# Attention, token shift and low-rank products of the first block, placed between the column tiles of the mixer's input projection

## What is computed

```
hn = rms_norm(h, g_mix[l]) * (1.0 + sc2) + sh2
proj = hn @ w_mix_in[l]                      # 1024 -> 2560 columns
p_att, p_rwkv, p_conv = split(proj, ...)     # 768, 1024 and 768 columns
y_att  = sliding_window_sink_attention(p_att, ...)   # 8 query heads, 2 key heads of 64
y_rwkv = rwkv7_time_mix(p_rwkv, ...)         # p = p + mu * (token_shift(p) - p), then a recurrence
y_conv = short_conv_mix(p_conv, conv_w)      # b_gate * conv3(c_gate * h)
h = h + (1.0 + gt2) * concat(y_att, y_rwkv, y_conv) @ w_mix_out[l]
```

## Time and profile before

| what | us |
|---|---|
| median of three runs | 3284.01 |
| the profiled execution, its own time | 3291.0 |
| its span, first to last instruction | 3288.9 |
| TensorE busy | 3033.3 (92%) |
| VectorE busy | 1597.2 (49%) |
| ScalarE busy | 977.7 (30%) |
| GpSimd busy | 228.7 (7%) |
| TensorE on the chain that ended last | 87% |

### The profile page before, as it was taken

One profiled execution on the slowest core, in us unless ns is written; L12 is line 12 of the kernel. 1 busy time (PEld: TensorE's weight loads), 2 busy tenths in 40 slices (PEclk: granted clock), 3 DMA queues, 4 the chain that ended last, 5 costly groups with the idle time before them and its releaser, 6 DMA issues.

```text
span 3288.9 us, 43744 instructions
## 1 busy us (share of the span) xinstructions
PE 3033.3 (92%) x18020; PEld 2377.0 (72%) x18020; DVE 1597.2 (49%) x2062; ACT 977.7 (30%) x1451; POOL 228.7 (7%) x286
## 2 busy tenths in 40 slices
PE   6999999959899998999999868999999999968996
PEld 5888877328688887888876357788877778748785
DVE  6676552355566624333342464433344545755533
ACT  3222222232322223222221322322333444523322
POOL 2000000401000000000004010000010000003000
PEclk8999999888999999999999978999999999968998
DMA  6565432000255522232221001223222112100121
GB/s 245 185 206 199 157 122 93 0 0 15 91 199 197 184 71 89 86 102 96 89 88 55 1 2 40 77 86 112 78 89 96 58 64 71 61 20 3 56 100 47
DMA packets 45366, 298.58 MB, mean 91 GB/s; under 512 B 5665, under 2 KB 5793, under 8 KB 16801
## 3 DMA queue, kind: packets, MB, share of 16 engines
q1 hardware_dynamic: 36000, 229.31, 20.5%
q0 software_dynamic: 9216, 67.11, 6.0%
HBM read 294.30 MB, written 2.10 MB: 90 GB/s over the span
## 4 chain that ended last, share of the span: by engine, by line
PE 87%; DVE 9%; ACT 2%; issue 1%; DMA 0%; POOL 0%; SPq 0%; DVEq 0%; ACTq 0%
PE ps L910 18%; PE ps L911 18%; PE ps L912 18%; PE ps L1091 3%; PE ps L1093 3%; PE ps L1092 3%; PE ps L1063 2%; PE ps L817 1%; PE ps L1396 1%; PE ps L1397 1%; PE ps L1398 1%; PE ps L1974 1%; PE ps L780 1%; PE ps L1958 1%; PE ps L1971 1%; PE ps L1174 1%
## 5 line engine op out<-in xcount | busy, mean ns | idle before, releaser
L910 PE MATMUL ps<-hn_hi,w_hi 128*128 128x512 f32 x1856 | 733.8, 395 | 47.7 <-DVE hn_lo L861 36.1
L911 PE MATMUL ps<-hn_lo,w_hi 128*128 128x512 f32 x1856 | 729.4, 393 | 0.0
L912 PE MATMUL ps<-hn_hi,w_lo 128*128 128x512 f32 x1856 | 728.9, 393 | 0.0
L887 DVE TENSOR_TENSOR w_lo<-w_raw,w_hi 128x2048 fp32r<-128x2048 f32 (+3 forms) x229 | 472.5, 2063 | 180.3 <-ACT w_hi L880 179.9
L910 PEld LDWEIGHTS ps<-hn_hi,w_hi 128*128 128x128 f32 x1856 | 353.1, 190 | 127.6 <-issue 54.6
L880 ACT ACTIVATE w_hi<-w_raw 128x2048 fp32r<-128x2048 f32 (+3 forms) x229 | 394.4, 1722 | 80.8 <-PE ps L1093 62.0
L911 PEld LDWEIGHTS ps<-hn_lo,w_hi 128*128 128x128 f32 x1856 | 352.9, 190 | 74.6 <-issue 1.8
L912 PEld LDWEIGHTS ps<-hn_hi,w_lo 128*128 128x128 f32 x1856 | 352.3, 190 | 73.9
L910 PE MATMUL ps<-act_hi,w_hi 128*128 128x512 f32 x704 | 289.5, 411 | 0.0
L911 PE MATMUL ps<-act_lo,w_hi 128*128 128x512 f32 x704 | 279.0, 396 | 0.0
L912 PE MATMUL ps<-act_hi,w_lo 128*128 128x512 f32 x704 | 278.4, 395 | 0.0
(11 more groups left out here) (453 smaller groups left out, 3915.0 us busy)
## 6 DMA issues: line engine op xcount, KB each, us to landing
w_raw<-in_up SPq DMA_DIRECT2D x88, 1024.0 KB, 4.9
ada_w<-in_ada POOLq DMA_DIRECT2D x64, 1024.0 KB, 5.1
w_raw<-in_down SPq DMA_DIRECT2D x64, 704.0 KB, 4.0
w_raw<-in_mix_in SPq DMA_DIRECT2D x20, 1024.0 KB, 4.9
w_raw<-in_dsa_in SPq DMA_DIRECT2D x18, 1024.0 KB, 5.0
w_raw<-in_merge SPq DMA_DIRECT2D x16, 768.0 KB, 4.3
ada_first<-in_ada SPq DMA_DIRECT2D x8, 1024.0 KB, 16.8
w_raw<-in_mix_out SPq DMA_DIRECT2D x8, 1024.0 KB, 4.9
```

The lines of the kernel that those rows point to most:

```text
L887: dve.tensor_tensor(w_lo[:, slot, 0:size], w_raw[:, slot, 0:size], w_hi[:, slot, 0:size].bitcast(F32), ALU.subtract).then_inc(w_lo_ready, 1)
L910: pe.matmul(bank, wh, x_hi[:, k], start=(k == 0), stop=False)
L911: pe.matmul(bank, wh, x_lo[:, k], start=False, stop=False)
L912: return pe.matmul(bank, wl, x_hi[:, k], start=False, stop=(k == K - 1))
```

## The change

The attention of the first block is issued in slots. A slot `at` is one column tile of the projection (24 products), from 0 to 19, and what TensorE does behind it. The scores of unit u stand in slot u + 7, its turning in slot u + 9, its product with the values in slot u + 10. The products with no use (`warm_pe`) are gone. `MIX_ORDER` changes the order of the column tiles, so that keys and values come first. The token shift goes from GpSimd to VectorE, in four parts in slots 9, 11, 13 and 15. The low-rank products come in slots 16 to 18, and the sums of `rw_kk` in slot 18. The convolution stays on GpSimd, but begins on each half when its tiles are there. The attention's result is written to `proj` first, and split into `hn_hi` and `hn_lo` after the projection, which still reads these. Many tiles get other places in memory; these lines are left out below.

```diff
-POOL_MIX = 21
+POOL_MIX = 12
+MIX_ORDER = (4, 5, 0, 1, 2, 3, 6, 7, 8, 9, 10, 11, 12, 13, 14, 15, 16, 17, 18, 19)
+ATT_SLOT = 7
...
 mix_pool:
-                own(pool.tensor_tensor(shift[:, :, 1:T], pr[:, :, 0:T - 1], pr[:, :, 1:T], ALU.subtract))
...
-                pool.tensor_tensor(pr, pr, shift[:], ALU.add).then_inc(shifted, 1)
...
+                    pool.wait_ge(act_evac, p0 + 8 + j)
+                    pool.wait_ge(dve_evac, p0 + 8 + j)
+                    u, y = proj[:, 14 + 2 * j], proj[:, 15 + 2 * j]
+                    own(pool.tensor_tensor(u, u, y, ALU.mult))
...
+                pool.wait_ge(act_evac, p0 + 10)
+                pool.wait_ge(dve_evac, p0 + 10)
+                pool.tensor_tensor(conv_y, conv_y, proj[:, 18:20], ALU.mult).then_inc(conv_ready, 1)
...
-        def warm_pe(pe, n):
...
+        def att_guests_pe(pe, l, at):
+            v, p0 = l + 1, start_of["mix_in", (l, 0)]
+            if at == 2:
+                pe.wait_ge(qk_squared, 3 * l + 1)
...
+                pe.matmul(ps[:, 7], blk[:], att_r[:, 4], start=True, stop=True).then_inc(qk_sums, 1)
+            if at == 3:
+                pe.wait_ge(dve_evac, p0 + 1)
...
+            if at == ATT_SLOT:
+                pe.wait_ge(qk_squared, 3 * l + 3)
+                pe.wait_ge(qk_roots, 2 * l + 1)
...
+                        last = pe.matmul(ps[:, 7, col:col + 2], att_r[:, j, n * P:(n + 1) * P], heads, start=True, stop=True)
+                last.then_inc(qk_sums, 1)
+            if 0 <= at - ATT_SLOT - 3 < 8:
+                att_pv_pe(pe, l, at - ATT_SLOT - 3)
+            if 0 <= at - ATT_SLOT - 2 < 8:
+                att_turn_pe(pe, l, at - ATT_SLOT - 2)
+            if 0 <= at - ATT_SLOT < 8:
...
+                att_scores_pe(pe, l, at - ATT_SLOT)
+            if at >= 16:
+                lora_pe(pe, l, at - 16)
+        def lora_pe(pe, l, step):
+            if step == 0:
...
+                pe.wait_ge(lora_ready, v)
+                pe.wait_ge(att_masked, 8 * v)
...
 mix_pe:
+            for i in range(MIX_TILES // 2):
+                narrow_pe(pe, p0 + i, (lambda k: pe.wait_ge(hn_ready, (3 * l + 1) * KD + k + 1)) if i == 0 else None, by_k=i == 0,
+                          guests=lambda t: att_guests_pe(pe, l, 2 * i + t))
...
 mix_act:
+            for at in range(MIX_TILES):
+                i = at // 2
+                if 0 <= at - ATT_SLOT - 3 < 8:
+                    turned(at - ATT_SLOT - 3)
+                if at % 2:
+                    m = MIX_ORDER[2 * i]
+                    first_evac_act(act, p0 + i, proj[:, m:m + 1])
+                else:
+                    split_act(act, *whole(p0 + i + 1))
...
+                if 0 <= at - ATT_SLOT - 4 < 8:
+                    out(at - ATT_SLOT - 4)
+                if 0 <= at - ATT_SLOT - 1 < 8:
+                    exps(at - ATT_SLOT - 1)
+                if at == 16:
+                    act.wait_ge(shifted, 4 * v)
+                    act.activation(proj[0:HD, 12], proj[0:HD, 12], ACT.Tanh)
...
+            act.wait_ge(piece_done, p_end)
+            act.wait_ge(att_out, 8 * v)
+            act.activation(hn_hi[:, 0:4], proj[:, 0:4], ACT.Copy).then_inc(att_out_hi, 1)
...
 mix_dve:
+            def shifts(i):
+                x = proj[:, 2 * i:2 * i + 2]
+                dve.wait_ge(act_evac, p0 + i + 1)
+                dve.wait_ge(dve_evac, p0 + i + 1)
+                dve.tensor_tensor(shift[:, :, 1:T], x[:, :, 0:T - 1], x[:, :, 1:T], ALU.subtract)
+                own(dve.tensor_scalar(shift[:, :, 0:1], x[:, :, 0:1], -1.0, None, ALU.mult))
+                for t in range(2):
+                    last = dve.scalar_tensor_tensor(x[:, t], shift[:, t], vcol(l, "mu", 2 * (i - 3) + t), x[:, t], ALU.mult, ALU.add)
...
+            for at in range(MIX_TILES):
+                i = at // 2
...
+                if 0 <= at - ATT_SLOT - 1 < 8:
+                    masked(at - ATT_SLOT - 1)
+                if at % 2 == 0:
+                    if i:
+                        evac(i - 1)
+                    split_dve(dve, *whole(p0 + i + 1))
...
+                if 0 <= at - ATT_SLOT - 2 < 8:
+                    divided(at - ATT_SLOT - 2)
+                if at in (9, 11, 13, 15):
+                    shifts((at - 3) // 2)
...
+                if at == 18:
+                    dve.wait_ge(gates_ready, 3 * l + 1)
...
+            evac(MIX_TILES // 2 - 1)
+            dve.wait_ge(gates_ready, 3 * l + 2)
             dve.wait_ge(kk_norms, v)
...
             last.then_inc(bonus_raw, 1)
+            dve.wait_ge(att_out_hi, v)
+            own(dve.tensor_tensor(hn_lo[:, 0:4], proj[:, 0:4], hn_hi[:, 0:4].bitcast(F32), ALU.subtract))
             dve.wait_ge(decays_ready, v)
```

More of the change, by code:

```diff
@@ L1075, in att_scores, with att_turn_pe, att_pv_pe @@
             last.then_inc(att_scored, 1)
+        def att_turn_pe(pe, l, u):
+            g, U = u % 2, 8 * l + u
+            pe.wait_ge(att_probs, U + 1)
+            if U:
+                pe.wait_ge(att_p_ready, U)
+            for kt in range(1 if u < 2 else 2):
+                for j in range(4):
+                    last = pe.transpose(ps[:, 4 + kt, j * P:(j + 1) * P], att_s[:, g, j, kt * P:(kt + 1) * P], ident[:])
+            last.then_inc(att_turned, 1)
+        def att_pv_pe(pe, l, u):
+            n, g, U = u // 2, u % 2, 8 * l + u
+            nk = 1 if n == 0 else 2
+            if u == 0:
+                pe.wait_ge(att_v_ready, l + 1)
+            pe.wait_ge(att_p_ready, U + 1)
+            if U >= 2:
+                pe.wait_ge(att_out, U - 1)
+            rows = half(g)
+            for kt in range(nk):
+                last = pe.matmul(ps[rows, 6], att_v[:, n + 1 - nk + kt, rows], att_p[:, kt], start=(kt == 0), stop=(kt == nk - 1))
+            last.then_inc(att_pv, 1)
@@ L1763, in mix_pe @@
             p0 = start_of["mix_in", (l, 0)]
-            def piece(i, odd):
-                def ready(k):
-                    if isinstance(i, int) and i == 0:
-                        pe.wait_ge(hn_ready, (3 * l + 1) * KD + k + 1)
-                pe_piece(pe, p0 + i, (p0 + odd) % 2, KD, 2, hn_hi, hn_lo, ready, by_k=isinstance(i, int) and i == 0)
-            steps(pe, MIX_TILES // 2, piece)
-            pe.wait_ge(qk_squared, v)
-            if l == 0:
-                pe.wait_ge(masks_ready, 1)
@@ L1812, in mix_pe @@
-            pe.wait_ge(lora_ready, v)
-            pe.wait_ge(att_out, 8 * v)
-            pe.wait_ge(lora_loaded, 16 * v)
-            for j in range(2):
-                cols = slice(j * P, (j + 1) * P)
-                pe.matmul(ps[:, 4 + j], lora[0:HD, 0, cols], proj[0:HD, 12], start=True, stop=True)
-                pe.matmul(ps[:, 6 + j], lora[HD:P, 0, cols], proj[HD:P, 12], start=True, stop=True)
-                last = pe.matmul(ps[:, j], lora[:, 1, cols], proj[:, 13], start=True, stop=True)
@@ L1826, in mix_pe @@
+            pe.wait_ge(act_evac, p0 + MIX_TILES // 2)
+            pe.wait_ge(dve_evac, p0 + MIX_TILES // 2)
+            pe.wait_ge(gates_ready, 3 * v)
             pe.wait_ge(bonus_raw, v)
@@ L2623, in mix_columns @@
     q = [HD * h + i for h in heads for i in range(HD)]
-    return np.array(q + list(range(len(q), MIX_TILES * P)))
+    columns = np.array(q + list(range(len(q), MIX_TILES * P)))
+    conv = len(q) + 2 * P + 8 * P
+    for at, tile in enumerate((2, 4, 3, 5, 0, 1)):
+        columns[conv + at * P:conv + (at + 1) * P] = np.arange(conv + tile * P, conv + (tile + 1) * P)
+    return np.concatenate([columns[m * P:(m + 1) * P] for m in MIX_ORDER])
 def mix_rows():
```

294 lines of the change are left out of this document (136 added, 158 removed).

## The result

The median of four executions is 3119.73 us (3116.16 to 3124.97), beside 3283.53 for the kernel before: ratio 0.951, 95% interval 0.949 to 0.952. That is 164 us less, inside the forecast's range of 3093 to 3130, and 14.7 us above the forecast of 3105. The profiled execution took 3116.16.

A forecast was written before the change was run, and what follows sets the result against it. No engine is full; the 171.0 and 166.4 us between projection and recurrence are a chain across engines. Less 44.7, 2.1 and 32.3 per layer, 91.9 and 87.3 are saved: 3284.0 - 179 = 3105, range 3093 to 3130.

The forecast's parts named there:

- What leaves the path: Stretch from the projection's last product to the recurrence's first: all 171.0 (layer 0) and 166.4 us (layer 1) go, with exceptions.
- Guests on TensorE: Small products placed between the projection's tiles add 44.7 us of work per layer, plus about 2 us of waits.
- The tile between guests at 5.44 us: In the projection, each tile's 24 products take 5.44 us of TensorE, also with small products between tiles.
- the clock is 1.00 between tiles if the projection keeps it: Premise for small products in the projection: at full clock query sums take 3.3 us, against 6.6 at 0.50.
- the second rival: Clock falls at slot 7's query sums and the waits of slots 10 to 14: +20 us, 3125; chance 12%.
- Behind the projection: Between projection and recurrence 32.3 us stay: bank copy 0.65, VectorE's chain 29.4, new low-part pass 2.3.
- Rivals 1, 3 and 4: VectorE sets the slot: 3153, 7%; clock 1.2 GHz from slot 2 to 19: 3391, 1.5%; no overlap: 3237, 2.5%.
- If the clock falls in slot 7: Sign of a wrong forecast: TensorE's clock, forecast at 1.00 in all slots, falls in the query sums' slot.
- the other two: Signs of a wrong forecast: slots longer than 11.5 us, or the stretch behind the projection over 36 us.
- The range's low end: 3093: no waits in the slots (-4), VectorE's new pass hidden (-5), better clock behind the projection (4.6 us).
- its forecast of 3112: Profiled execution of 3291.0 us less 179; the median of the runs was taken 7.0 lower.

The follow-up runs named there:

- experiment 5: Changed kernel with all small products issued behind the 20 tiles, copies and splits before the attention, so no overlap; 3200.92 us, ratio 0.975.
- experiment 3: Changed kernel with the 16 query sums in four places of four products: slots 5, 6, 7 and the middle of tile 8; 3110.67 us.
- experiments 6 and 8: Changed kernel: low-part pass behind the last factor, 3114.57 us; last bank's copy behind the first scaling and convolution's last step on VectorE, 3110.95 us.

## Why the prediction was right, and where it missed

- **What leaves the path**, 171.0 and 166.4: right. Nothing of it is left but what was named. What it did not see is that half of this was to be had without the overlap (experiment 5); that did not enter the sum.
- **Guests on TensorE**, 44.7 of work and 2.1 of waits, 46.8 together. Added up from TensorE's timeline, from each guest's start to the next tile's, they are 46.4 in layer 0 and 47.0 in layer 1, where 0.6 is the first scores at the low clock. Inside: query sums 3.6 (forecast 3.3), the two narrow scores 2.2 with their switches (1.6), waits 1.0 (2.1). VectorE was not sooner than forecast: in slot 12 it ended the division 7.8 us behind the tile's start (7.7 forecast), but TensorE wanted it only at 7.6 and not at 7.2, since the tile and the product with the values took 0.4 us more. The sizes hold.
- **The tile between guests at 5.44 us**: the step that failed, in two ways. First, "the clock is 1.00 between tiles if the projection keeps it": it kept it through the waits and the scores, but not behind the query sums. Tile 8 took 1.8 and 2.8 us more than 5.44, and the scores in layer 1 0.6 more: 5.2 together, some 0.4 of it switches (experiment 3 won 4.5 back, with three more visits a layer paid). That is the second rival in kind and place (slot 7), at a quarter of its price of 20. Of its two reasons the waits were wrong: the Trainium skill's rule that cycling through banks with short stops lets the clock swing ("TensorE: Matmul & The Clock Gate", section "A second HAM failure mode: psum-queue depth-cycling") does not show here, with two banks and waits of up to 0.6 us at 1.00 from 520 to 600; the fall came where TensorE never stopped. Second, the change between large and small products, 0.2 us for each tile between guests, 2.6 a layer, stood nowhere in the sum. I had checked the second block for gaps, and its slot of 11.38 has the switches inside: its tile's 24 products took 5.98 us, from 2577.43 to 2583.41; 0.4 us of the excess lie right behind a small product of 512 columns, as they do in tile 3 of this stage. Only the total was used, as evidence of no gaps. The remaining 1.1 us of layer 0 are in the projection's first two and last tiles; in layer 1 these add nothing.
- **Behind the projection**, 32.3: measured 32.6 and 32.8. The 0.69 of the copy, the chain and the 2.28 of the new pass are there one for one; experiments 6 and 8 show the new pass and the wait for the bank on the path. It had room: the chain waited for a bank that it did not need.
- **Rivals** 1, 3 and 4 did not occur: VectorE is idle for 2.2 to 3.1 us before each wide mask, the clock was low behind slot 7 for 3.4 and 6.8 us of 164, and the wide slots are 9.7 to 10.8 us.
- **Signs and bounds.** "If the clock falls in slot 7" was one of the prediction's own signs of being wrong, and it came; the other two did not. The time stayed in the range because the fall was short. The range's low end is not the sum of its terms: 3105 - 4 - 5 - 4.6 is 3091.4, not 3093.
- **From profile to median.** The profiled execution came 4.2 us above its forecast of 3112: 12.1 too much gain in the stage, less 7.4 gained elsewhere; the rest is rounding and the edges of the span. The median is 3.6 above the profiled execution, where I took it 7.0 below. Those 10.6 are the larger part of the miss of 14.7: which execution the profiler caught, on either side. The 7.4 elsewhere were luck and hid part of the 12.1.

## What to carry to other kernels

Before an overlap is built, run the rebuilt chain alone, behind the large products: here half the gain lay there. When small products move between large ones, price the switch (0.2 us a visit here), and spread runs of very small products, because a busy TensorE can still lose its clock behind them. When a freed engine gives less than its idle time, look at what the moved work now lies beside: GpSimd's step took 2.0 us from VectorE in three of four places.

## What was not expected

- TensorE's granted clock fell to 1.2 GHz with no idle time in front of it, behind 8 to 16 products of 2 columns (3.6 us for 16); with four in one place never.
- 16 query sums took 3.56 us at 1.00, where they took 6.6 at 0.50: even products of 2 columns go nearly with the clock.
- One product of 128x1024 on GpSimd stops VectorE for 2.0 us, whether a copy of 128x16 or a full product is held up, but not its reciprocal of 6.55 us.
- The clock in the tail was 0.58 (TensorE busy for 8.6 us of 32.5) and in the tail of experiment 5 0.65, against 0.84 and 0.87 before; both were faster. What a higher clock would have been worth there was not measured.

```profile
618.60:651.10 32.50, 8.60 (x28) 5.78 (x28) 27.52 (x22) 9.95 (x9) 2.63 (x1) 0.58 0.00 0
```
